# Both halves of the scatter ahead of the transposes in a mixture-of-experts stage

## The reference

```
def moe_ffn(h, router_w, router_b, w_gate, w_up, w_down, sh_gate, sh_up, sh_down):
    scores = jax.nn.sigmoid((xf @ router_w).astype(F32))
    ...                                     # group-limited choice of 6 of 64 experts
    topw = topw / (jnp.sum(topw, -1, keepdims=True) + 1e-20) * ROUTED_SCALE
    routed = routed_experts(xf, topi, topw, w_gate, w_up, w_down)
    shared = (jax.nn.silu(xf @ sh_gate) * (xf @ sh_up)) @ sh_down
    return (routed + shared).reshape(B, S, D)

# routed_experts, for each block of rows that belongs to one expert e:
        xb = xf[rt]
        hb = jax.nn.silu(xb @ w_gate[e]) * (xb @ w_up[e])
        yb = (hb @ w_down[e]).astype(F32) * rw[:, None]
        return acc.at[rt].add(yb), None
```

## Time and profile before

| | |
|---|---|
| median of 3 runs | 2144.76 us |
| lowest and highest | 2141.98 and 2148.73 us |
| the profiled execution | 2148.73 us |
| its span | 2146.9 us |
| TensorE busy | 93% of the span |
| VectorE, ScalarE busy | 43%, 16% |
| mean granted TensorE clock | 0.957 of 2.4 GHz |
| DMA | 576.91 MB, mean 269 GB/s |

### The profile page before, as it was taken

The page is one execution under the profiler, slowest core; times in us unless marked ns, Lnnn a source line. Parts: engine busy times, 40 slices in busy tenths (PEclk is TensorE's granted clock), DMA queues, the critical chain, the costliest instruction groups (busy, mean ns, idle before and its releaser), DMA issues.

```text
span 2146.9 us, 23408 instructions
## 1 busy us (share of the span) xinstructions
PE 2002.3 (93%) x9094; PEld 1210.9 (56%) x9094; DVE 933.6 (43%) x1905; ACT 345.8 (16%) x870; POOL 84.5 (4%) x101
## 2 busy tenths in 40 slices
PE   5999999999999989999969999999999896879988
PEld 4886644433433378899656444343333784638855
DVE  5555734222222147678656442222221546342164
ACT  1122111111111123300121111111110303021121
POOL 0100000000000000000000000000000000020031
PEclk9999999999999989999969999999999998879999
DMA  9863588899999845522446889999998771203301
GB/s 406 316 239 123 235 352 353 361 423 423 423 421 423 345 177 216 181 95 99 180 159 254 348 353 373 422 424 423 422 423 356 299 289 34 76 3 101 134 26 40
DMA packets 82108, 576.91 MB, mean 269 GB/s; under 512 B 9148, under 2 KB 11452, under 8 KB 12800
## 3 DMA queue, kind: packets, MB, share of 16 engines
q1 hardware_dynamic: 70992, 494.84, 56.9%
q0 software_dynamic: 10992, 80.43, 10.3%
HBM read 574.17 MB, written 1.06 MB: 268 GB/s over the span
## 4 chain that ended last, share of the span: by engine, by line
PE 86%; DVE 9%; DMA 2%; issue 1%; ACT 1%; POOL 1%; DVEq 0%; SPq 0%; POOLq 0%
PE ps L301 84%; DVE hma L514 2%; PE ps L305 2%; DMA wbuf<-in_ada 1%; ACT slab L308 1%; DVE slab L313 1%; DVE wbuf L480 0%; DVE hma L313 0%; DVE slab L1252 0%; DVE gds L651 0%; DMA slab<-in_ada 0%; DVE slab L312 0%; DVE stat L2314 0%; DVE slab L2048 0%; POOL rs_t L2459 0%
## 5 line engine op out<-in xcount | busy, mean ns | idle before, releaser
L301 PE MATMUL ps<-slab 128*128 128x256 f32 (+7 forms) x1936 | 575.9, 468 | 10.0 <-DVE slab L2331 8.1
L301 PE MATMUL ps<-wbuf,slab 128*64 128x512 f32 (+2 forms) x1584 | 437.0, 593 | 0.1
L301 PEld LDWEIGHTS ps<-slab 128*128 128x128 f32 (+2 forms) x1936 | 290.6, 181 | 222.2 <-issue 203.9
L301 PE MATMUL ps<-hma,wbuf 128*128 128x256 f32 (+1 forms) x1648 | 375.6, 390 | 0.9 <-DVE hma L313 0.9
L301 PEld LDWEIGHTS ps<-hma,wbuf 128*128 128x128 f32 (+1 forms) x1648 | 318.9, 195 | 50.8 <-issue 4.9
L301 PEld LDWEIGHTS ps<-wbuf,slab 128*64 128x64 f32 (+1 forms) x1584 | 148.4, 145 | 240.1 <-issue 238.9
L308 ACT ACTIVATE slab<-ps 128x256 f32<-128x256 f32 (+3 forms) x145 | 66.2, 464 | 1177.4 <-PE ps L301 1176.4
L301 PE MATMUL ps<-wbuf,cst 128*64 128x512 f32 x704 | 190.8, 592 | 0.0
L1530 DVE TENSOR_TENSOR slab<-ps,rs_t 128x512 f32<-128x512 f32 x128 | 88.5, 691 | 216.9 <-PE ps L301 216.9
L301 PE MATMUL ps<-wP,slab 128*64 128x512 f32 (+2 forms) x440 | 160.3, 486 | 12.5 <-DVE wP L2307 8.9
L1518 DVE TENSOR_TENSOR slab<-ps,slab 128x256 f32<-128x256 f32 x64 | 27.2, 424 | 324.7 <-ACT slab L308 324.5
(11 more groups left out here) (275 smaller groups left out, 1588.4 us busy)
## 6 DMA issues: line engine op xcount, KB each, us to landing
wbuf<-in_moe_gu SPq DMA_DIRECT2D x170, 1024.0 KB, 9.0
wbuf<-in_moe_d SPq DMA_DIRECT2D x88, 1024.0 KB, 10.5
slab<-in_moe_gu SPq DMA_DIRECT2D x64, 1024.0 KB, 9.5
wbuf<-in_ada POOLq DMA_DIRECT2D x60, 1024.0 KB, 5.3
wbuf<-in_od_in SPq DMA_DIRECT2D x30, 1024.0 KB, 4.8
wbuf<-in_ev_in SPq DMA_DIRECT2D x22, 1024.0 KB, 8.4
wP<-in_moe_gu SPq DMA_DIRECT2D x22, 1024.0 KB, 9.5
slab<-in_moe_d SPq DMA_DIRECT2D x20, 1024.0 KB, 10.7
```

The costliest lines, as they stand in the source:

```text
L301: return e.matmul(o, lhsT, rhs, start=start, stop=stop, skip_group_check=skip)
```

## The change

The two calls of `scatter_pe` for a pair, one for each half m of the tokens, stood on either side of the transposes. Now one call does both halves, ahead of the shared slice and the transposes. The function loops over m itself, and it waits once, for the second half of `m_ys`, instead of for each half. The event m_y comes, as before, with the last of its matmuls. The matmuls, their operands and the order in which each bank accumulates are the same. After the last pair both halves stood together already.

```diff
--- before.py
+++ after.py
@@ -1312,17 +1312,17 @@
                     t = afn(e, m_xl[q % 2][:, k:k + v.shape[1], 64 * i:64 * i + 64], v[:, :, bass.ds(b, 64)], ACT.Copy)
             t.then_inc(*C.up("m_xl", l, q))
 
-        def scatter_pe(e, l, q, m):
-
-            for f in range(2):
-                e.wait_ge(*on("m_ysc", l, q, f))
-                t = mm(e, YT(m, f), m_tp[:, q % 2, 256 + m * 128:384 + m * 128], m_ys[:, q % 2, f * 512:f * 512 + 512],
-                       False, q == NP - 1, True)
-                if q == NP - 1:
-                    t.then_inc(*P.up("y_out", f"m{l}", m, f))
-            if m and q < NP - 1:
+        def scatter_pe(e, l, q):
+            e.wait_ge(*on("m_ysc", l, q, 1))
+            for m in range(2):
+                for f in range(2):
+                    t = mm(e, YT(m, f), m_tp[:, q % 2, 256 + m * 128:384 + m * 128], m_ys[:, q % 2, f * 512:f * 512 + 512],
+                           False, q == NP - 1, True)
+                    if q == NP - 1:
+                        t.then_inc(*P.up("y_out", f"m{l}", m, f))
+            if q < NP - 1:
                 t.then_inc(*P.up("m_y", l, q))
-            elif m:
+            else:
                 P.also("m_y", l, q)
 
         def moe_sp(e, l, before):
@@ -1427,7 +1427,7 @@
                             P.also("used", ("m_w", l, x, k0))
                 P.also("m_gu", l, q, 1)
                 if q:
-                    scatter_pe(e, l, q - 1, 0)
+                    scatter_pe(e, l, q - 1)
                 if 0 <= q - SHARED_AT < 8:
                     shared_pe(e, l, q - SHARED_AT)
                 p = fill_bank(e, ("m_tt", l, q), ("m_ttc", l, q))
@@ -1438,8 +1438,6 @@
                 for m in range(2):
                     t = tr(e, p[:, 256 + m * 128:384 + m * 128], m_PW[g % 2][:, m, o:o + 128])
                 t.then_inc(*P.up("m_tt", l, q))
-                if q:
-                    scatter_pe(e, l, q - 1, 1)
                 if q + 3 < 2 * NC:
                     gather_pe(e, l, q + 3)
                 for half in range(2):
@@ -1459,8 +1457,7 @@
                                 if half == 1:
                                     P.also("used", key)
                     P.also("m_ys", l, q, half)
-            for m in range(2):
-                scatter_pe(e, l, NP - 1, m)
+            scatter_pe(e, l, NP - 1)
             over(e, l, over_pe, P)
 
         def moe_act(e, l):
```

## The result

The changed kernel takes 2181.26 us (median; 2179.41 to 2185.17) against 2144.8 us (2141.98 to 2148.73) before: a ratio of 1.0183, 95% interval 1.0166 to 1.0202, which is 36 to 43 us more. It is slower, as forecast, and the time lies in the lower part of the range. The profiled execution has a span of 2187.1 us against 2146.9 us, 40.2 us more.

A forecast was written before the change was run, and what follows sets the result against it. TensorE, busy 93% of the span, was taken to pace the kernel. 46 pairs x 0.98 us (1.51 - 2.25 + 1.72) = 45.1 us on the 2144.76 us median gave 2189.8 us, range 2178 to 2207 us.

The forecast's parts named there:

- The new distance: From a pair's first transpose to its first down matmul: set by VectorE's copy, 1.51 us against 2.25 us before.
- release and restart: TensorE resuming after VectorE's copy: 0.15 us for release and 0.03 us for restart, taken from pair 0.
- Its waiter is of the same form: Pair 0's wait gave the 0.15 us release, being also a weight load taking a VectorE result.
- the range's lower bound: Resuming after the copy costs nothing: 1.33 us of distance, 0.80 us per pair, 36.8 us in all, 2181.6 us.
- 46 pairs: Expert pairs q = 9 to 31, without gathers, 23 in each of two layers: each 0.98 us longer.
- gather steps unchanged: Pairs 1 to 8 cost nothing, as gathers remain between transposes and down; their steps stay 17.97 us.
- shared ones as the plain ones: Pairs with a shared expert slice lengthen too: steps about 16.4 us, plain pairs about 15.5 us.
- the single wait free: One m_ysc wait ahead of both scatter halves costs nothing: the previous down ends about 7 us earlier.
- the copy was expected by name: TensorE's waits should show release by the L1523 copy 46 times, 0.9 us each, 40 us in all.
- A, the weights: Weight transfers pace the expert stage, swallowing 0.35 us per pause in 30 plain pairs: 2179.4 us; chance 0.03.
- B, the clock: TensorE's clock falls to 1.2 GHz over each down group behind a pause: 158 us more, 2349 us; chance 0.05.
- C, the front wait: If transposes waited for m_hh, moved work would fill that pause: not slower, 2144.8 or 2139 us; chance 0.03.

The follow-up runs named there:

- the copy in two: Changed kernel with VectorE's copy of the transposes split, the 256 columns for the down matmuls first: 2168.12 us, ratio 1.0118 to the kernel before.
- the copy three times: Kernel before with VectorE's copy of the transposes made three times, each waiting for the last: 2169.95 us, ratio 1.0115.
- the shared slice: Changed kernel with the shared expert's slice moved behind the transposes: 2172.11 us, ratio 1.0144 to the kernel before.
- three and one: Changed kernel with three of the four scatter matmuls ahead of the transposes and one behind: 2147.25 us, ratio 1.0018 to the kernel before.
- both halves behind: Changed kernel with both scatter halves behind the transposes, none in front: 2198.24 us, ratio 1.0247 to the kernel before.
- the repeat: Changed kernel, unaltered, timed again beside the kernel before: 2185.57 us against 2141.82 us, ratio 1.0194.
- the kernel without the scatter: Changed kernel without the scatter of pairs 0 to 30, so part of the output is missing: 2108.95 us (one run).
- the kernel with the single wait: Kernel before with only one wait, for the second half of m_ys, ahead of the first scatter half: 2142.14 us, ratio 0.9994.
- the kernel with the places later: Kernel before with VectorE's lists of places computed at the end of an even pair, no longer ahead of m_hh: 2136.81 us, ratio 0.9961.

## Why the prediction was right, and where it was off

*The new distance.* The mechanism was right: the distance from the first transpose to the down matmuls is now that of the copy. Two experiments tie it to the copy's end (the copy in two, the copy three times), one shows that other work covers as well (the shared slice), and one shows the threshold (three and one).

*Its size.* The term that was mis-sized is release and restart: 0.15 + 0.03 us taken from the transposes of pair 0, where 0.10 us was measured. No restart shows at all: 1.43 + 1.72 - 2.25 us is the measured 0.90 us with nothing left over. The waits of the two forms differ, and did in every kernel: the copies end at 440.70, 439.02 and 438.03 and the down matmuls start 0.10, 0.10 and 0.11 us later, while the product in the kernel with both halves behind ends at 451.71 and its transposes start 0.16 us later. So the distance is 1.43 us and not 1.51, 0.90 us per pair and not 0.98, 41.4 us and not 45.1. The difference lies ahead of the weight load: it begins 0.07 us behind the copy (440.77) but 0.12 us behind the product, and the first matmul follows the load by 0.03 to 0.04 us in both. Why down's load is released sooner no run tells; it is 64 columns wide and the transposes' 128. "Its waiter is of the same form", the prediction's ground for 0.15 us, was an assumption, and it did not hold.

*How near the edge.* The sum went by 0.98 us and the range's lower bound by 0.80 us per pair, 2181.6 us in all; 0.90 us is well between them. Yet the first median, 2181.26 us, is below that bound and inside the range only by the 3 us allowed for scatter. That the median came so low is scatter between executions: the repeat and all executions together give 2184.5 to 2185.6 us.

*The steps around it.* 46 pairs; gather steps unchanged; shared ones as the plain ones; the single wait free, if for the last pair of a layer not for the reason given: all as forecast. In the table of waits the copy was expected by name and stood as "issue".

*Rivals.* A, the weights: its 2179.4 us is nearer to the first median than the forecast's 2189.8 us, so the time alone could not reject it. The steps do: the lengthening came in full, 0.90 us in plain pairs as well as in shared ones, so nothing was swallowed; the kernel without the scatter shows that such a limit exists, at 14.83 us. The Trainium skill ("DMA: Bandwidth & Descriptors", Where 436 GB/s comes from) gives 435 GB/s as the ceiling of the fabric, from which the prediction estimated 14.46 us per pair; the same section says that for transfers between HBM and SBUF a lower limit of about 358 GB/s binds. The 50 us window shows 424 GB/s, between the two, and the measurement decides. B, the clock: 1.00 in the window with four pauses, and steps of one length throughout (the prediction's 2349 us for it should be 2348 us). C, the front wait: it exists once its cover is gone (1.06 us in the kernel with both halves behind), and was covered before, with the room that the rows gave.

## What to carry to other kernels

Independent work on a busy engine is also cover for the hand-over to another engine and back. Before moving it, measure for each gap how long the hand-over takes and what is left to cover it: up to that point a move is free, beyond it the whole shortfall is paid in every turn. In this kernel two gaps of about 1 us (the pauses are 0.83 and 1.06 us when bare), each with 1.7 us of cover, were right as they were; 3.4 us of cover in one place, whichever, cost 41 or 53 us.

## What was not expected of the hardware

The wait of 3.34 us in pair 0 can be followed by a stretch at TensorE's lower clock. Windows of 4 us from the first transpose of pair 0 in layer 1 show it. The kernel before:

```profile
1163.82:1167.82 4.00, 4.00 (x12) 3.37 (x13) 0.69 (x1) 0.00 (x0) 0.00 (x0) 0.50 1.03 434
```

The kernel with the single wait:

```profile
1157.20:1161.20 4.00, 4.00 (x20) 3.32 (x20) 1.69 (x3) 0.00 (x0) 0.00 (x0) 1.00 1.02 430
```

The kernel with the places later:

```profile
1153.95:1157.95 4.00, 4.00 (x20) 3.32 (x20) 1.69 (x3) 0.00 (x0) 0.00 (x0) 1.00 1.01 426
```

In the profiled execution of the kernel before, the clock is 0.50, the 1.2 GHz level, and 12 matmuls start in the time of 20; in that of the kernel with the single wait, which waits as long there (3.35 us), it is 1.00. In the chain the 68 records from there take 18.24 us in the one and 15.82 us in the other, and the four transposes ahead of them 1.09 for 0.63 us: 2.9 us together. The changed kernel's profile shows the low clock at the same place.

How often it happens the other profiles tell. Ten profiles on record have a wait of 3.3 us in pair 0 of both layers. At 10 of these 20 places the granted clock is 0.50 to 0.67 in the 4 us from the first transpose, and the step to the next turn is 1.7 to 2.9 us longer than the same step at full clock, 2.4 us in the mean; at the other 10 it is 1.00. That would be about 2.4 us per execution. Behind the wait of 1.06 us in the kernel with the places later the clock is at 1.00 in both layers, but two places are too few to show that the shorter wait prevents the fall. If it does, 4.6 and 2.4 us make 7 us of the 8 us gained. The 46 pauses of 0.83 us never lowered the clock: every plain step of the changed kernel's profile is 15.41 or 15.42 us.

At least as much of the scatter between runs lies elsewhere. From the last turn of the first layer to the first of the second, the kernel before took 416.9 us and the kernel with the single wait 410.4 us, with lower clocks in the former (0.83, 0.83 and 0.80 for 0.86, 0.88 and 0.82 in the three 50 us windows from 1000 us); what sets them there was not looked into.
